# First loads of each stage issued from within the stage before it, with stage buffers taken in turns from both ends of SBUF

## The reference, cut to what matters

```
h = x @ w_in                                   # u, v (gMLP), q, k, v (8 heads), memory q, 3 gates
g_out  = u * (tril(W_s) @ LN(gelu v) + b_s)    # chunks of 128 tokens
sb_out = stick-breaking attention(q, k, v)     # strictly causal, no softmax
m_out  = softmax attention into 256 memory tokens
mix = (sum_b sigmoid(gate_b) * branch_b @ w_br_b) @ w_out
x = LN1(alpha * x + mix)
x = LN2(alpha * x + PEER(x))
```

## Time and profile before

| what | us |
|---|---|
| median of 3 runs | 4849.47 (4844.11 to 4852.52) |
| the profiled execution | 4842.91 |
| its span in the profile | 4841.2 |
| PE busy / DVE busy in it | 3289.7 / 3157.7 |
| ACT busy / POOL busy | 993.4 / 1372.4 |
| mean DMA rate | 326 GB/s, 1579.68 MB |

### The profile page before, as it was taken

The page is one execution under the profiler, slowest core; times in us unless marked ns, Lnnn a source line. Parts: engine busy times, 40 slices in busy tenths (PEclk is TensorE's granted clock), DMA queues, the critical chain, the costliest instruction groups (busy, mean ns, idle before and its releaser), DMA issues. The chain is left out here.

```text
span 4841.2 us, 38032 instructions
## 1 busy us (share of the span) xinstructions
PE 3289.7 (68%) x10576; PEld 1748.2 (36%) x10576; DVE 3157.7 (65%) x6031; ACT 993.4 (21%) x2018; POOL 1372.4 (28%) x1287
## 2 busy tenths in 40 slices
PE   8679786455987687446455556985904777777776
PEld 6466542333544333334211112432401333333322
DVE  0121277896767688889766665887687666766754
ACT  1120111243211110235323231221101111111121
POOL 0000023322223234312111112332234454444432
PEclk9789898566998899567666667997957998989989
DMA  5343489777989899866799998998879999999988
GB/s 212 103 138 144 161 326 372 284 251 283 360 329 374 313 369 399 295 221 223 287 412 408 407 399 307 378 360 326 351 247 372 421 421 421 421 421 421 421 359 335
DMA packets 311757, 1579.68 MB, mean 326 GB/s; under 512 B 36536, under 2 KB 96108, under 8 KB 155823
## 3 DMA queue, kind: packets, MB, share of 16 engines
q0 software_dynamic: 158288, 1151.42, 60.1%
q1 hardware_dynamic: 122750, 377.41, 20.5%
q10 hardware_dynamic: 30560, 49.03, 2.7%
HBM read 1526.49 MB, written 50.99 MB: 326 GB/s over the span
## 5 line engine op out<-in xcount | busy, mean ns | idle before, releaser
L1600 POOL DMA_INDIRECT peer_row<-in_peer_uv,peer_staged x640 | 776.8, 1214 | 2112.2 <-DVE peer_y L1805 2013.4
L1789 DVE SCALAR_TENSOR_TENSOR peer_row<-peer_row,peer_x 128x1024 f32<-128x1024 f32 x640 | 779.9, 1219 | 183.4 <-DMA peer_row<-in_peer_uv,peer_staged 151.3
L1805 DVE SCALAR_TENSOR_TENSOR peer_y<-peer_row,peer_coef,peer_y 128x1024 f32<-128x1024 f32 x640 | 817.9, 1278 | 0.0
L1968 PE MATMUL tail_y<-peer_row,tail_diag 128*128 128x512 f32 x896 | 441.2, 650 | 308.5 <-ACT tail_diag L1981 308.5
L1968 PE MATMUL tail_y<-tail_row,tail_diag 128*128 128x512 f32 x896 | 432.8, 641 | 130.9 <-ACT tail_diag L1981 130.9
L245 PE MATMUL pr_b<-pr_xT,pr_w 128*128 128x256 f32 (+2 forms) x1152 | 389.8, 502 | 110.0 <-DMA pr_xT<-in_xT 79.2
L829 PE MATMUL gs_gp<-gs_xT,gs_w 128*128 128x256 f32 (+2 forms) x1152 | 393.5, 496 | 51.1 <-DMA gs_w<-in_w_gate 46.2
L1968 PEld LDWEIGHTS tail_y<-peer_row,tail_diag 128*128 128x128 f32 x896 | 181.7, 208 | 567.2 <-issue 384.8
L1927 POOL DMA_INDIRECT peer_row<-in_peer_uv,tail_staged x224 | 259.3, 1158 | 307.1 <-PE tail_y L1968 237.0
L1927 POOL DMA_INDIRECT tail_row<-in_peer_uv,tail_staged x224 | 253.3, 1131 | 281.0 <-PE tail_y L1968 245.0
L245 PEld LDWEIGHTS pr_b<-pr_xT,pr_w 128*128 128x128 f32 x1152 | 225.6, 197 | 272.7 <-issue 180.3
(11 more groups left out here) (216 smaller groups left out, 4350.9 us busy)
## 6 DMA issues: line engine op xcount, KB each, us to landing
sa_kc<-in_cache_k SPq DMA_DIRECT2D x128, 512.0 KB, 14.4
sa_vc<-in_cache_v SPq DMA_DIRECT2D x128, 512.0 KB, 12.9
pr_w<-in_w_in SPq DMA_DIRECT2D x27, 2048.0 KB, 10.9
gs_w<-in_w_gate SPq DMA_DIRECT2D x36, 1024.0 KB, 9.6
rt_w<-in_w_q SPq DMA_DIRECT2D x24, 1024.0 KB, 8.8
gs_w<-in_w_br SPq DMA_DIRECT2D x24, 512.0 KB, 5.0
gs_w<-in_w_br SPq DMA_DIRECT2D x12, 1024.0 KB, 7.8
mx_w<-in_w_out SPq DMA_DIRECT2D x6, 2048.0 KB, 12.3
```

The costliest lines, as they stand in the source:

```text
L1600: pool.indirect_dma_start(out=self.row[b][:], out_offset=None, in_=dr["peer_uv"], in_offset=bass.IndirectOffsetOnAxis(ap=self.staged[slot] ...
L1789: v.scalar_tensor_tensor(out=self.row[b][:, 0:D], in0=self.row[b][:, 0:D], scalar=1.0, in1=self.x1[:], op0=ALU.mult, op1=ALU.mult, accum_o ...
L1805: v.scalar_tensor_tensor(out=self.y[:], in0=self.row[b][:, D:2 * D], scalar=self.coef[:, col:col + 1], in1=self.y[:], op0=ALU.mult, op1=AL ...
L1968: done = pe.matmul(part[:], diag[r % (2 * ROWS)][:], row[place(j, k)][:, D + hf * 512:D + (hf + 1) * 512], start=j == 0 and k == 0, stop=j ...
```

## The change

Each stage but `attend_sample` gets a class that holds its first buffers and the semaphores of its first loads (`ProjectAhead`, `LocalAhead`, `PromptAhead`, `SumAhead`, `MixAhead`, `RouteAhead`). The object for a stage is made before the stage ahead of it runs, and SP issues its `load` from within that stage. To let both stages' buffers live at once, `Phase` takes a side, and successive stages take their buffers from the right and the left end of SBUF in turns. Not everything moves: the tiles of `local_branches`, brT in `gated_sum`, x and the constants in `mix_and_norm` are still loaded in their own stage, and so are mkT and mv in group 0. Of w_out 4, 3 and 1 of four parts move in groups 0, 1 and 2. The first block of w_in moves in groups 0 and 1, xT in all three. In group 2 `attend_prompt` hands nothing on, `attend_sample` is as before, and `gated_sum` loads everything itself. No matmul, activation or vector instruction is added or taken away.

```diff
-    def __init__(self, nc, name):
-        self.nc, self.name, self.ctx = nc, name, ExitStack()
+    def __init__(self, nc, name, side="left"):
+        self.nc, self.name, self.side, self.ctx = nc, name, side, ExitStack()
...
+class ProjectAhead:
...
+    def load(self, sp):
+        sp.dma_start(self.xT[:], self.dr["xT"][:, :, self.cols]).then_inc(self.x_loaded, 16)
+        if self.with_weights:
+            sp.dma_start(self.w0[:], self.dr["w_in"][0]).then_inc(self.w0_loaded, 16)
...
             for u in range(units):
-                if u == 1:
-                    sp.dma_start(xT[:], dr["xT"][:, :, t0:t0 + T]).then_inc(x_loaded, 16)
+                if u == 0 and own.with_weights:
+                    continue
...
                 sp.dma_start(wbuf[u % 2][:], src).then_inc(w_loaded[u % 2], 16)
+            following.load(sp)
...
+class LocalAhead:
...
+    def load(self, sp):
+        dr = self.dr
+        for dst, src in ((self.tril[:], dr["tril"]), (self.ws[:], dr["w_spatial"]), (self.lng[:], dr["gln_g"]),
+                         (self.lnb[:], dr["gln_b"]), (self.ones[:], dr["ones"]), (self.bs[:], dr["b_spatial"]),
+                         (self.ident[:], dr["ident"])):
+            sp.dma_start(dst, src).then_inc(self.const_loaded, 16)
+        if self.g:
+            self.load_memory(sp)
...
                 fetch(n)
+                if n == 1:
+                    following.load(sp)
...
+class PromptAhead:
...
+    def load(self, sp):
+        for h in range(self.HR):
+            self.load_head(sp, h)
+            if h == 0:
+                for dst, src in ((self.neg[:], "neg"), (self.ident[:], "ident"), (self.bias[:], "sb_bias")):
+                    sp.dma_start(dst, self.dr[src]).then_inc(self.const_loaded, 16)
...
+            for h in range(HR, HEADS):
+
+                sp.wait_ge(summed, last_piece[(h - HR + 1) * tiles - 1] + 1)
+                own.load_head(sp, h)
+            if following:
+                following.load(sp)
...
+class SumAhead:
...
+    def load(self, sp):
+        sp.dma_start(self.xT[:], self.dr["xT"][:, :, self.cols]).then_inc(self.x_loaded, 16)
+        self.load_weights(sp, 0)
+        self.load_weights(sp, 1)
+        sp.dma_start(self.bgate[:], self.dr["b_gate"]).then_inc(self.bias_loaded, 16)
...
+            if not own.loaded_ahead:
+                own.load(sp)
...
+                own.load_weights(sp, u)
+            following.load(sp)
...
+class MixAhead:
...
+    def load(self, sp):
+        for i in range(self.n_parts):
+            self.load_part(sp, i)
...
-            for c in range(2):
-                sp.dma_start(w[:, c], dr["w_out"][c]).then_inc(w_loaded[c], 16)
+            for i in range(own.n_parts, 4):
+                own.load_part(sp, i)
...
                 sp.dma_start(dst, dr[src]).then_inc(const_loaded, 16)
+            following.load(sp)
...
+class RouteAhead:
...
+    def load(self, sp):
+        for u in range(3):
+            self.load_weights(sp, u)
+        sp.dma_start(self.keysT[:], self.dr["keysT"]).then_inc(self.keys_loaded, 16)
...
+            for u in range(3, 8):
+                sp.wait_ge(query_ready, per_unit * (u - 2))
+                own.load_weights(sp, u)
+            if following:
+                following.load(sp)
...
+MIX_PARTS_AHEAD = (4, 3, 1)
...
+        sides = cycle(("right", "left"))
...
+            local_own = LocalAhead(nc, next(sides), sem("local"), dr, g)
+            project(nc, block, sem("project"), dr, bg, g, tile0, tiles, project_own, local_own)
             gate.close(block)
```

More of the change, by code:

```diff
@@ L13 @@
 from contextlib import ExitStack
+from itertools import cycle
 import concourse.bass as bass
@@ L355, in _ @@
             fetch(0)
[L356 to L360, removed]
+            if g == 0:
+                own.load_memory(sp)
             def keep(n):
@@ L895, in mix_and_norm @@
         const_loaded = sem("ln1_loaded")
-        w_loaded = [sem(f"wo_loaded{i}") for i in range(2)]
         x_loaded = sem("x_loaded")
@@ L936, in _ @@
                     for k in range(KD):
-                        last = pe.matmul(mix_ps[j % 4][:], zT[:, k, n * P:(n + 1) * P], w[:, c, k, :],
+                        part, kk = 2 * c + k // 4, k % 4
+                        if n == 0 and kk == 0:
+                            pe.wait_ge(w_loaded[part], 16)
+                        last = pe.matmul(mix_ps[j % 4][:], zT[:, k, n * P:(n + 1) * P], w[part][:, kk, :],
                                          start=k == 0, stop=k == KD - 1)
@@ L2093, in sem_of, with front, merged @@
             return sem
-        def front(block, made, gate, own, bg, g, tile0, tiles):
+        sides = cycle(("right", "left"))
+        def front(block, made, gate, own, bg, g, tile0, tiles, project_own, project_next):
             def sem(stage):
                 return sem_of(own, f"g{g}_{stage}", made)
+            T = tiles * P
+            cols = slice(tile0 * P, tile0 * P + T)
+            chunks = [(c, min(512, T - c)) for c in range(0, T, 512)]
             prompt_tiles = min(tiles, PT - tile0)
-            project(nc, block, sem("project"), dr, bg, g, tile0, tiles)
+            sampling = prompt_tiles < tiles
+            def merged(side):
+                whole = Phase(nc, f"mg{g}", side)
+                zT = whole.sb("zT", [P, KD, T])
+                return whole, zT, SumAhead(nc, side, sem("merge"), dr, g, tile0, tiles, not sampling)
+            local_own = LocalAhead(nc, next(sides), sem("local"), dr, g)
+            project(nc, block, sem("project"), dr, bg, g, tile0, tiles, project_own, local_own)
@@ L2110, in front @@
-            merge(nc, block, sem("merge"), gate, dr, bg, g, tile0, tiles)
+            if sampling:
+                attend_prompt(nc, block, sem("prompt"), dr, bg, g, tile0, prompt_tiles, prompt_own, None)
+                gate.close(block)
+                attend_sample(nc, block, sem("sample"), dr, bg, next(sides))
+                gate.close(block)
+                whole, zT, sum_own = merged(next(sides))
+            else:
+                whole, zT, sum_own = merged(next(sides))
+                attend_prompt(nc, block, sem("prompt"), dr, bg, g, tile0, prompt_tiles, prompt_own, sum_own)
+                gate.close(block)
@@ new lines, in front @@
+            mix_own = MixAhead(nc, next(sides), sem("merge"), dr, g, MIX_PARTS_AHEAD[g])
+            gated_sum(nc, block, sem("merge"), dr, bg, g, T, cols, chunks, zT, sum_own, mix_own)
+            gate.close(block)
+            route_own = RouteAhead(nc, next(sides), sem("merge"), dr, g)
+            mix_and_norm(nc, block, sem("merge"), dr, bg, g, tile0, tiles, zT, mix_own, route_own)
+            gate.close(block)
+            project_following = project_next(next(sides))
+            route(nc, block, sem("merge"), dr, bg, g, tile0, tiles, chunks, zT, route_own, project_following)
@@ L2119, in build, with project_ahead, make, _ @@
                 gate = Gate(sem_of(own, "gate", lasting)("passed"))
+                def project_ahead(g):
+                    def make(side):
+                        if g == len(GROUPS):
+                            return None
+                        return ProjectAhead(nc, side, sem_of(own, f"g{g}_project", lasting), dr, g, starts[g],
+                                            GROUPS[g]["tiles"], g < 2)
+                    return make
+                coming = project_ahead(0)(next(sides))
+                @block.sync
+                def _(sp):
+                    coming.load(sp)
                 for g, group in enumerate(GROUPS):
@@ L2124, in build @@
                         made = []
-                        front(block, made, gate, front_own, bg, g, starts[g], group["tiles"])
+                        coming = front(block, made, gate, front_own, bg, g, starts[g], group["tiles"], coming,
+                                       project_ahead(g + 1))
                         @block.sync
```

224 lines of the change are left out of this document (117 added, 107 removed).

## The result

| what | us |
|---|---|
| before, median of 4 runs | 4846.79 (4842.35 to 4852.52) |
| changed kernel, median of 4 runs | 4761.70 (4760.80 to 4762.97) |
| ratio, 95% interval | 0.9824 (0.9807 to 0.9841) |
| the profiled executions, before and after | 4842.91 and 4760.80 |
| their spans | 4841.2 and 4759.1 |

The change makes the kernel 1.8% faster, 82.1 us between the profiled executions. The forecast was 4768, from 81 us. PE is busy for 3287.7 us and DVE for 3156.8, against 3289.7 and 3157.7 before: no work went, only waits. The mean granted clock of TensorE is 0.825, against 0.815 before.

What follows compares the result with a forecast made beforehand. Bound by PE or DVE idling behind stage gates until loads land, with DVE often last in groups 1 and 2. Gains of 97 us minus 16 for moved loads give 81: median 4768 us, own range 4737 to 4805, 8-in-10 range 4722 to 4824.

Steps and rivals of the forecast that it cites:

- Group 0: Gains in group 0's prompt (5.0), sum (7.5), mix (9.0) and route (4.7) from waits behind gates: 26.2 us.
- Prompts: attend_prompt of groups 1 and 2: first score starts about at the gate, gaining 7.7 and 8.6 us.
- Routes: route of groups 1 and 2: PE starts about at the gate, gaining 7.5 and 7.2 us.
- Sum of group 1: gated_sum of group 1: branch product about 14.5 us after the gate instead of 24.7, gain 10 us.
- mix of group 1: mix_and_norm of group 1: DVE's wait of 28.4 us falls to 15.5 plus 1, gain 12 us.
- Project of group 2: project of group 2: xT ahead lets PE start some 15 us earlier, about covering DVE's 15.82 us stall; gain 14.
- Mix of group 2: mix_and_norm of group 2: only 1 MB of 7.06 moves, gain 3.5 us.
- The charge of 16 us: Cost of moved loads beside DVE's background gathers: project 6, 3 for each mix, 4 for group 1's route.
- the upper bound of 37 us: Greatest cost of moved loads: all 14.4 MB falling where DVE is ready to work, charged at 394 GB/s.
- B: Rival: groups 1 and 2 pay every moved byte in full, 27.8 MB, 71 us; time 4823; chance 0.14.
- C: Rival: without pauses POOL's ring of eight rows is not refilled, DVE meets late gathers; slower, 4899; chance 0.06.
- D: Rival: earlier starts also save PE's slow first products, 3.1 us in nine stages, 28 us more; 4740; chance 0.08.

Runs made afterwards that it cites:

- second experiment: Changed kernel with loads issued ahead only within group 0 and for group 1's first stage: 4817.21 us, ratio 0.9940 to the kernel before.
- fifth experiment: Changed kernel whose background in groups 1 and 2 fetches only the u half of each expert row, no longer computing the layer: 4613.76 us, one run.
- sixth experiment: Kernel with buffers from both ends and all loads in their own stage, except group 2's project xT issued ahead: 4840.85 us, one run.
- third experiment: Changed kernel with route's first loads (4 MB) issued at the start of route again, in all groups: 4779.59 us, ratio 0.9858 to the kernel before.
- the seventh: Changed kernel with local_branches' constants, mkT and mv loaded behind its gate again in groups 1 and 2: 4766.37 us, ratio 0.9829 to the kernel before.
- eighth experiment: Changed kernel with route's keys fetched four times in sequence during the mix, 3 MB more per group: 4776.44 us, ratio 0.9845 to the kernel before.
- first experiment: Changed kernel with its buffers and split semaphores kept, but no stage's loads issued ahead: 4847.66 us, ratio 1.0009 to the kernel before.

## Why the prediction was right, point by point

The mechanism is the one predicted: waits behind gates go, and the stages shorten by them. The time came out where it was expected, though, because two of its errors were of about the same size, which is luck. The stages with a predicted gain gave 85.4 us of 96.7, net of what their own moved loads cost. The stages without one (project of groups 0 and 1, the local branches, sample, the sum of group 2 and the tail) lost 3.3 together, mostly 2.7 in attend_sample, which is within its spread. 85.4 - 3.3 = 82.1. So 11 us of gain were missing, and about 13 of the 16 us charged.

- **Group 0**, 26.2 predicted: 26.1. Prompt 4.0 for 5.0, sum 7.2 for 7.5, mix 9.8 for 9.0, route 5.6 for 4.7. DVE's first product of the mix came 8.4 us after the gate, 9 to 10 were predicted. Shown alone by the second experiment.
- **Prompts** of groups 1 and 2, 7.7 and 8.6: 8.1 and 8.1. **Routes**, 7.5 and 7.2: 4.8 and 8.2. In group 1's route PE starts as early as predicted, but DVE's stalls for the gelu stay (the row at 1449.10, 4.20 us; such waits total 13.7 us in that stage before and 14.8 after), so a part of the earlier start is not DVE's.
- **Sum of group 1**, 10 predicted, 7.6 measured, and **mix of group 1**, 12 predicted, 7.2 measured: here the step failed, as a size. The prediction scaled the wait by the front's bytes, from 6.6 to 3.6 MB, and added 1 or 2 us for the gathers. By the DMA records of the trace 6.9 MB of loads and 4.6 MB of gathers moved in the 28.4 us before DVE's first product of the mix; in the changed kernel 4.3 and again 4.6 in 21.3 us (the loads hold 0.7 MB of what SP issues next). The gathers do not shrink with the loads: whatever POOL issued by the gate, and the few that the ring's free buffers allow after it, must go through as well. 28.4 x (4.3 + 4.6) / (6.9 + 4.6) = 22.0 is what the measured 21.3 follows, and not 16. In the sum, likewise, 2.1 MB of gathers moved before and after: 24.7 x (3.5 + 2.1) / (6.8 + 2.1) = 15.5, measured 16.1, predicted 14.5. The fifth experiment tests this with gathers of half the size: 28.4 x (4.4 + 2.1) / (6.9 + 4.6) = 16 for the mix, measured 17.1. The gathers are the other part.
- **Project of group 2**, 14: 12.2, by xT alone (sixth experiment). PE starts 12.2 us after the gate, the 15.8 us stall of the earlier trace rows is gone. DVE's waits for rows in this stage grow from 28.9 to 33.1: a part of the stall became a wait for rows. In the other kernels with xT ahead and whole rows those waits are 33.7 to 43.8 us and the stage 321.8 to 327.9, so by these executions the load is worth 5 to 12 us, and the 14 were too many.
- **Mix of group 2**, 3.5: 2.6; DVE starts 28.4 us after the gate, 27 predicted.
- **The charge of 16 us.** 3 for each mix is not there, by the third experiment; 3 for group 1's project is there by the seventh, and given back in local_branches; the stage's own xT and first weights, which came ahead too and which the prediction put at nothing, hide a part of it (250.1 us in the second experiment, where these loads alone are ahead of it, 252.8 before). The 4 for the route does not show in its row waits, which fell from 17.4 to 12.5 us in group 1. The total of DVE's waits for rows, predicted to grow by 16, fell by 1.6; with no load ahead it was 142.1 us in the first experiment's execution and 151.3 in that of the kernel before, so changes of 10 us are within its spread. The sizes in the code make the 14.4 MB some 15.0, and the 394 GB/s are not the limit (below): the upper bound of 37 us would be 36 at 421 GB/s. Neither changes a chance.

**The rivals.** B wanted those waits to grow by 50 us and more; they did not, and B is out. The Trainium skill's rule on queues that take turns ("DMA: Bandwidth & Descriptors", Queues, rings and completion order) is not against the trace: in the full window behind the mix's gate the two queues moved 4.6 and 4.3 MB. Taking turns cost DVE little in the mix, which at 0.90 had room. In the eighth experiment, at 0.97, the room is all but gone.

C wanted gathers that land towards 15 us in the stages. Those issued behind the gate of group 1's mix, and those after, landed in:

```profile
DMA to landing us min/median/max: 9.7/11.0/12.3
```

```profile
DMA to landing us min/median/max: 5.7/6.9/8.2
```

Against 15.1 and 5.9 before, so DVE met its rows hardly later. The first of each pair is a median of three gathers. D fell too: the first gate product of group 1's sum still takes 7.57 us where the second takes 5.55, so 2.0 of the 3.1 us of the earlier trace rows stayed. The granted clock shows why: over the first product it was 0.64 before and is 0.71, over the second 1.00 and 0.96. By the trace's clock records it fell to the lower of its two levels (1.2 GHz of 2.4) at 1087.6, in a pause of PE of 4.5 us in the prompt, and rose at 1128.6, within the first product. It fell again at 1135.4, while PE waited 8.19 us for brT, so the branch product takes 5.46 us at 0.50 where it took 4.27 at 0.64. The earlier start did not save here what the clock costs.

That the gain is the time of issue is shown by the first experiment, to within its interval and with the two differences in group 0 told there.

## What to carry to other kernels

To price the bytes that stay behind a gate, count all queues that run then, background gathers included: taking two fifths to a half of the front's own bytes away took only a quarter to a third off the wait. Loads moved into an earlier stage cost about nothing here where that stage's DMA share stayed clear of 1, which its window tells beforehand; where it was full, they were paid there (3 us in the one case seen here, given back by the stage that they left). The one reordering tried behind a gate moved the wait to the next operand and left group 1's stage as long; a load cut into parts, so that the first product can start on the first part, did shorten a stage with all its loads behind the gate (3.4 us in group 0's mix, first experiment).

## What the runs showed of the hardware that was not expected

- With gathers and loads in flight together the core moved 418 GB/s for 21.4 us (the window at 1360.3), above the 394 that the prediction took as what is possible. The page of the kernel before already had more, in seven of its 40 slices, in the tail; the prediction did not use that row:

```profile
GB/s 212 103 138 144 161 326 372 284 251 283 360 329 374 313 369 399 295 221 223 287 412 408 407 399 307 378 360 326 351 247 372 421 421 421 421 421 421 421 359 335
```

- A stage took 4.1 MB more beside its gathers in 0.4 us more (307 against 357 GB/s in group 1's mix), and 3 MB on top of that came with 1.1 us (391 GB/s, share 0.97): in this stage a price shows only close to the full share, and that from one execution of each kernel.
